# The latent-attention stage of a two-layer kernel in another order: one block projection ahead of the first scores, the first rotations shared by two engines, banks and steps dealt otherwise

## The reference, cut to what matters

```python
proj = u @ ab_w_in[e]                        # c_q | c_kv | k_rope_in | block q, k, v
q  = rmsnorm(c_q, q_norm_g) @ w_uq           # per head 64 plain + 32 rotated columns
kv = rmsnorm(c_kv, kv_norm_g) @ w_ukv        # per head 64 key + 64 value columns
q_rope, k_rope = rope(q[..., 64:], pos), rope(k_rope_in, pos)   # k_rope is shared by all heads
def rope(x):  # x1, x2: the halves of the 32 columns
    return concat([x1 * cos - x2 * sin, x1 * sin + x2 * cos])
logits = (q_nope @ k_nope.T + q_rope @ k_rope.T) * scale       # causal
out = softmax(logits) @ v                    # then @ ab_w_out, feed-forward, layer 1 (stick-breaking), feed-forward
```

## Time and profile before

| | us |
|---|---|
| median of the runs | 1307.0 |
| lowest, highest | 1306.68, 1309.34 |
| the profiled execution, its own time | 1307.3 |
| its span, first to last instruction | 1305.5 |
| PE busy in the span | 1266.4 |
| mean granted clock of TensorE | 0.991 |
| latent stage, first query product of head 2 to scores 7 (62.79 to 151.50) | 88.7 |
| PE busy in that stretch | 74.3 |

### The profile page before, as it was taken

The page is one execution under the profiler, slowest core; times in us unless marked ns, Lnnn a source line. Parts: engine busy times, 40 slices in busy tenths (PEclk is TensorE's granted clock), DMA queues, the critical chain, the costliest instruction groups (busy, mean ns, idle before and its releaser), DMA issues.

```text
span 1305.5 us, 17382 instructions
## 1 busy us (share of the span) xinstructions
PE 1266.4 (97%) x6487; PEld 1067.4 (82%) x6487; DVE 723.8 (55%) x928; ACT 553.0 (42%) x883; POOL 217.5 (17%) x198
## 2 busy tenths in 40 slices
PE   6979899999999999999999999999999999999997
PEld 5767788889888888888898888888988888888885
DVE  4677655528545545422258889884765545452223
ACT  5456666546422222222246565565542222232112
POOL 1532200026111111100042000002521111110002
PEclk9989999999999999999999999999999999999999
DMA  5412222132333333333322221213133333332331
GB/s 165 127 52 59 79 73 73 38 92 66 113 97 96 96 96 96 89 102 91 93 77 65 64 66 55 74 49 97 58 105 97 96 96 97 97 114 93 89 90 65
DMA packets 190502, 112.33 MB, mean 86 GB/s; under 512 B 13696, under 2 KB 184773, under 8 KB 190446
## 3 DMA queue, kind: packets, MB, share of 16 engines
q1 hardware_dynamic: 188636, 106.81, 28.2%
q0 software_dynamic: 640, 2.10, 0.6%
q10 hardware_dynamic: 1170, 2.66, 0.5%
HBM read 109.43 MB, written 4.74 MB: 87 GB/s over the span
## 4 chain that ended last, share of the span: by engine, by line
PE 85%; DVE 8%; ACT 3%; issue 2%; POOL 1%; DMA 0%; POOLq 0%; ACTq 0%; DVEq 0%; SPq 0%
PE banks L432 27%; PE banks L434 26%; PE banks L433 26%; PE banks L1724 1%; PE banks L1631 1%; DVE w_lo L427 1%; PE banks L1455 1%; PE banks L1695 1%; DVE logits L1417 1%; ACT logits L1428 1%; DVE tf L698 1%; DVE probsT_lo L1467 1%; POOL residual L769 0%; DVE stick_lo L1708 0%; DVE u_lo L708 0%
## 5 line engine op out<-in xcount | busy, mean ns | idle before, releaser
L427 DVE TENSOR_TENSOR w_lo<-w_raw,w_hi 128x1024 fp32r<-128x1024 f32 (+3 forms) x200 | 289.8, 1449 | 272.5 <-ACT w_hi L420 272.3
L432 PE MATMUL banks<-u_hi,w_hi 128*128 128x512 f32 (+1 forms) x1112 | 424.1, 381 | 5.6 <-DVE w_lo L427 4.3
L434 PE MATMUL banks<-u_hi,w_lo 128*128 128x512 f32 (+1 forms) x1112 | 419.9, 378 | 0.0
L433 PE MATMUL banks<-u_lo,w_hi 128*128 128x512 f32 (+1 forms) x1112 | 419.8, 377 | 0.0
L420 ACT ACTIVATE w_hi<-w_raw 128x1024 fp32r<-128x1024 f32 (+3 forms) x200 | 206.6, 1033 | 262.0 <-PE banks L434 261.7
L432 PEld LDWEIGHTS banks<-u_hi,w_hi 128*128 128x128 f32 x1112 | 211.0, 190 | 44.5 <-issue 3.9
L434 PEld LDWEIGHTS banks<-u_hi,w_lo 128*128 128x128 f32 x1112 | 211.0, 190 | 38.5
L433 PEld LDWEIGHTS banks<-u_lo,w_hi 128*128 128x128 f32 x1112 | 211.1, 190 | 36.7
L901 POOL TENSOR_TENSOR up<-up,gate 128x512 f32<-128x512 f32 x44 | 71.9, 1634 | 375.7 <-DVE up L927 358.3
L882 ACT ACTIVATE gate<-gate 128x512 f32<-128x512 f32 x44 | 27.8, 632 | 202.3 <-DVE gate L923 202.3
L602 POOL TENSOR_TENSOR sq_sum<-sq_sum,sq_tile 128x512 f32<-128x512 f32 x14 | 18.4, 1317 | 362.6 <-ACT block_out L583 362.6
(11 more groups left out here) (246 smaller groups left out, 1807.6 us busy)
## 6 DMA issues: line engine op xcount, KB each, us to landing
w_raw<-in_ffn_w_gate_up_dram SPq DMA_DIRECT2D x88, 512.0 KB, 3.7
w_raw<-in_ffn_w_down_dram SPq DMA_DIRECT2D x30, 512.0 KB, 3.6
w_raw<-in_sb_w_qkv_dram SPq DMA_DIRECT2D x24, 512.0 KB, 3.7
w_raw<-in_ab_w_in_dram SPq DMA_DIRECT2D x17, 512.0 KB, 3.7
w_raw<-in_ffn_w_down_dram SPq DMA_DIRECT2D x16, 448.0 KB, 3.6
w_raw<-in_ab_w_out_dram SPq DMA_DIRECT2D x8, 512.0 KB, 3.8
w_raw<-in_sb_w_out_dram SPq DMA_DIRECT2D x8, 512.0 KB, 3.8
bias_by_distance<-bias_rows ACTq DMA_DIRECT2D x1, 2560.0 KB
```

The lines of the kernel that those rows point to most:

```text
L427: dve.tensor_tensor(wl[:, c.slot, 0:w], raw[:, c.slot, 0:w], wh[:, c.slot, 0:w].bitcast(F32), ALU.subtract).then_inc(w_lo, 1)
L432: nc.tensor.matmul(o, lh, rh, start=start, stop=False, skip_group_check=True)
L433: nc.tensor.matmul(o, lh, rl, start=False, stop=False, skip_group_check=True)
L434: return nc.tensor.matmul(o, ll, rh, start=False, stop=stop, skip_group_check=True)
```

## The change

It touches the latent stage alone; from step 5 on the items of PE stand as before.

1. The first block projection, ("bq", 4), called x0, moves from slot b of step 0 to ahead of scores 0. ("bk", 4) and ("bq", 5) move to slot c of steps 0 and 2, step 4 has none, and the values' projection comes to slot b. The queries of head 2 move from ahead of scores 0 to behind it. The chunks are loaded in the new order.
2. The first three rotations (shared key part, heads 0 and 1) are shared: POOL keeps the product with cos, DVE takes the product with sin and the sum.
3. The shared key part is rotated and split once, on rows 64 to 95; ACT copies both parts to rows 32 to 63 of the two buffers for odd heads. Before, POOL wrote both row ranges, ACT rounded three times and DVE subtracted three times.
4. The keys of the two heads of a pair are rounded and subtracted apart (`odd_key_act`, `odd_key_dve`), the odd one later, with semaphores of their own.
5. Banks of the first eight items: 7, 3, 4, 5, 6, 3, 4, 7.
6. In steps 0, 2, 4 (`latent_step`) and 1, 3 (`keys_of`) ACT and DVE do the same work in another order: exponentials of head hh+1 come behind the keys where keys are due, and the rounding of the probabilities ahead of them.

The diff, cut:

```diff
-    names = [("cq", 0), ("ck", 0)]
-    for p in range(1, MLA_PAIRS):
-        names += [("cq", p), X_IN_LATENT[p - 1], ("ck", p)]
+    names = []
+    for p in range(MLA_PAIRS):
+        names += [("cq", p), ("ck", p)] + ([X_IN_LATENT[p]] if p in X_IN_LATENT else [])
...
-            steps.append([g[2], block_item(X_IN_LATENT[p]), g[3]])
+            steps.append([g[2], g[3], block_item(X_IN_LATENT[p + 1]) if p + 1 in X_IN_LATENT else None])
...
+    items = [q0, k0, q1, v0, x0, q2, vt0, k1] + [it for step in steps for it in step if it is not None]
+    vector_items = [k0, q0, q1, vt0, x0, k1, q2]
...
+        def rope_sin_dve(dve, number, rows=ROPE_ROWS):
+            dve.wait_ge(rp_sw, number + 1)
+            nc.vector.tensor_tensor(rt[rows, 0, :], rt[rows, 0, :], cs[rows, 1, :], ALU.mult).then_inc(rp_sin, 1)
+        def rope_sum_dve(dve, x, number, rows=ROPE_ROWS):
+            dve.wait_ge(rp_cos, number + 1)
+            dve.wait_ge(rp_sin, number + 1)
+            nc.vector.tensor_tensor(x[rows, :], rt[rows, 0, :], rt[rows, 1, :], ALU.add).then_inc(rp_done, 1)
...
-            return (7, 3, 4, 5, 6, 3, 7)[n] if n < 7 else P_BANK
+            return (7, 3, 4, 5, 6, 3, 4, 7)[n] if n < 8 else P_BANK
...
 (ACT, ahead of the steps)
+            load_functions(act, EXP_SET)
             act.wait_ge(rp_done, 1)
+            act.activation(mq[2][ROPE_ROWS, 0, :], k_rope[ROPE_ROWS, :], ACT.Copy).then_inc(kr_hi, 1)
+            item_act(act, k0)
+            item_act(act, q0)
+            odd_key_act(act, k0)
+            item_split_act(act, v0)
+            act.wait_ge(kr_lo, 1)
+            for b in (1, 2):
+                act.activation(mq[2][ODD_ROPE, b, :], mq[2][ROPE_ROWS, 0, :].bitcast(F32), ACT.Copy)
+                act.activation(mq[3][ODD_ROPE, b, :], mq[3][ROPE_ROWS, 0, :].bitcast(F32), ACT.Copy)\
+                    .then_inc(kr_odd, 1)
+            item_split_act(act, x0)
+            item_act(act, q1)
             exp_act(act, 0)
+            item_act(act, vt0)
             norm_act(act, 0)
...
 (ACT, steps 0, 2, 4)
+                if latent_step(hh):
+                    probs_act(act, hh)
+                    if keys_of(hh - 1):
+                        exp_act(act, hh + 1)
+                    norm_act(act, hh + 1)
+                    item_act(act, a)
+                    item_split_act(act, b)
+                    item_split_act(act, c)
+                    exp_act(act, hh + 2)
+                    item_act(act, c)
...
 (DVE, steps 0, 2, 4)
+                if latent_step(hh):
                     item_scale(dve, a)
+                    probs_dve(dve, hh)
+                    item_split_dve(dve, slots_of_step(hh - 1)[0] if hh else q2)
+                    den_dve(dve, hh + 1)
+                    item_scale(dve, b)
+                    if hh and not keys_of(hh - 1):
+                        o_dve(dve, hh // 2 - 1)
+                    scores_dve(dve, hh + 2)
+                    odd_key_dve(dve, keys_of(hh - 1))
+                    item_lo(dve, a)
+                    item_split_dve(dve, b)
+                    item_split_dve(dve, c)
+                    item_scale(dve, c)
+                    item_lo(dve, c)
...
 (PE, ahead of the steps)
-            for n in (2, 3, 5):
-                item_pe(pe, items[n])
+            for it in (q1, v0, x0):
+                item_pe(pe, it)
             scores_pe(pe, 0)
-            item_pe(pe, items[4])
+            item_pe(pe, q2)
+            item_pe(pe, vt0)
             scores_pe(pe, 1)
-            item_pe(pe, items[6])
+            item_pe(pe, k1)
```

More of the change, by code:

```diff
@@ L1156, in rope_rows_pool @@
             nc.gpsimd.tensor_tensor(rt[rows, 1, :], x[rows, :], cs[rows, 0, :], ALU.mult).then_inc(rp_cos, 1)
+        def rope_rows_pool(pool, x, number, scaled, rows=ROPE_ROWS):
+            rope_cos_pool(pool, x, number, scaled, rows)
             pool.wait_ge(rp_sw, number + 1)
@@ L1272, in keys_first, with latent_step, keys_of @@
             return (c, b) if b is not None and b[0] == "mq" else (b, c)
+        def latent_step(hh):
+            return hh % 2 == 0 and hh < 2 * MLA_PAIRS - 2
+        def keys_of(hh):
+            c = slots_of_step(hh)[2] if hh >= 0 else k1
+            return c if c is not None and c[0] == "mk" else None
         def item_split_act(act, it):
@@ L1299, in item_act @@
                 act.wait_ge(pj_read, read_at[it[:3]])
-                for rows, b in mk_dst(p):
-                    ins = act.activation(mq[2][rows, b, :], scaled_tile(it)[rows, :], ACT.Copy)
-                ins.then_inc(pj_hi, 1)
+                rows, b = mk_dst(p)[0]
+                act.activation(mq[2][rows, b, :], scaled_tile(it)[rows, :], ACT.Copy).then_inc(pj_hi, 1)
                 return
@@ L1363, in item_lo, with odd_key_act, odd_key_dve @@
             nc.vector.tensor_tensor(lo, scaled_tile(it)[rows, :], hi.bitcast(F32), ALU.subtract).then_inc(pj_lo, 1)
+        def odd_key_act(act, it):
+            rows, b = mk_dst(it[1])[1]
+            act.activation(mq[2][rows, b, :], scaled_tile(it)[rows, :], ACT.Copy).then_inc(k_odd_hi, 1)
+        def odd_key_dve(dve, it):
+            rows, b = mk_dst(it[1])[1]
+            dve.wait_ge(k_odd_hi, it[1] + 1)
+            nc.vector.tensor_tensor(mq[3][rows, b, :], scaled_tile(it)[rows, :], mq[2][rows, b, :].bitcast(F32),
+                                    ALU.subtract).then_inc(k_odd_lo, 1)
         def item_pool(pool, it):
@@ L2122, in _ @@
                     item_split_act(act, a)
-                if hh + 2 < NH0:
+                if hh + 2 < NH0 and not keys_of(hh):
                     exp_act(act, hh + 2)
```

157 lines of the change are left out of this document (79 added, 78 removed).

## The result

The changed kernel took 1297.4 us in the median of six runs (1295.98 to 1297.95), the kernel before 1307.3 beside it: a ratio of 0.992 with an interval of 0.9907 to 0.9934. It is faster, as forecast, but by 9.9 us and not by 14.8, and 1297.4 lies 0.9 us above the range. The profiled execution took 1295.98.

What follows compares the result with a forecast made beforehand. PE's waits on the chain product, scale, rotate, round, subtract, with DVE in every link, bound the stage; 68.6 us of work, 4.5 of waits and restarts gave a 14.8 us gain: 1307.0 - 14.8 = 1292.2, range 1289.5 to 1296.5.

Steps and rivals of the forecast that it cites:

- bound of 20.1 us: 88.7 us from head 2's queries to scores 7, less 68.6 at full speed: the most any order can give.
- 2.7 us booked for the clock: Scores 0 and 1 of the kernel before: time lost in all by running at a granted clock of 0.5.
- The start: Up to scores 0: operands ready 1.7 us earlier, scores 0 at 68.05 behind x0 without a wait, at full clock.
- The step that failed: Head 2's queries to scores 1: queries end 72.05, transposition 72.4, scores 1 74.35, the wait of 2.23 us gone.
- rival B: The clock falls again at waits of 0.5 and 1.9 us around pair 1's keys, costing 1.5: 1293.7 us; chance 0.23.
- Waits that are left: PE waits: pair 1's keys 0.5, probabilities 0 1.9, scores 2 0.2, probabilities 5 1.4, scores 7 0.5; together 4.5 us.
- The port: Two-input DVE instructions that meet POOL run in turns; if merely shared, a weight part ends 0.5 earlier: 1291.8 us.
- Steps 1 to 4: Waits of 0.66, 0.73 and 1.17 us go, a step pair lasts 22.85; probabilities 5 wait 1.4.
- rival C: Hand-offs slower than laid: narrowly avoided waits return and POOL wins another turn in step 4, 5.1 us: 1297.3; chance 0.20.
- D: Little gained: ACT stands at the chunk for q2 and k1, loaded three us late: 1295 us; chance 0.03.
- E: Slower than before: waits of steps 0 to 4 keep PE at 1.2 GHz, up to 1342 us; chance 0.03.
- PE without waits after: Behind scores 7: no new wait of PE, as in the old trace, so the whole gain arrives at the end.

Runs made afterwards that it cites:

- b1: The kernel before, with eight idle products on PE ahead of scores 0 and eight ahead of scores 1; 1308.0 us.
- e1: The changed kernel, but the transposition of pair 0's values waits only for the read of its own tile, not for x0's scaling; 1294.3 us.
- e7: The changed kernel with its wait kept and fourteen idle products on PE inside it, ahead of the transposition of pair 0's values; 1295.0 us.
- e8: e1 with DVE scaling the next query product behind the reading of the scores again in steps 1 and 3; 1296.0 us.
- e10: e1 with the two keys of a pair rounded and subtracted together again, as before the change; 1296.1 us.
- e6: The changed kernel with e1's edit, x0 scaled first, reciprocals earlier, step 4's weight part later and head 6's exponentials later on ACT; 1292.3 us.
- e9: e6 with the weight part of the chunk behind moved after the values' halves on ACT and DVE in the last steps; 1289.9 us.
- e11: e5 with 16 idle products on PE ahead of scores 1, inside its wait of 4.72 us; 1294.2 us.
- b2: The kernel before, with DVE scaling the next query product ahead of reading the scores in odd steps; 1311.3 us.
- e5: e1 with x0 back in its step: block projections in steps 0, 2 and 4, head 2's queries again ahead of scores 0; 1296.0 us.
- e2: The changed kernel with its wait kept, but DVE scales x0 ahead of head 2's queries; 1291.8 us.

## Why the prediction was wrong, point by point

- **What bounds the kernel, and the most that can be won.** The reading of the earlier trace rows held: most of what went is waiting (9.0 of 11.6 us). The bound of 20.1 us is the stage less its work at full clock, and it stands. But its parts are no prices of their own: the 2.7 us booked for the clock bring nothing when they alone are taken away (b1: 0.0 at x5), since a wait beside them takes them up.
- **The start.** Right: scores 0 at 68.49 behind x0 without a wait and at full clock (68.05 forecast; the stage began 0.33 later here). The sin products and sums on DVE took 0.68 us each, near the lower bound of 0.61 that was taken and far from 1.9. DVE reached the read of scores 0 at 70.57 and not at 69.2, since q1's sum and the odd key stood ahead of it; probabilities 0 come 0.5 late in e1 (23.63 against 78.3 - 55.2 = 23.1), and this is the likely cause; no run isolates it.
- **The step that failed** is this one: "The queries of head 2 run 70.0 to 72.05, the transposition to 72.4, scores 1 to 74.35." The queries of head 2 did end near there (72.59, with the stage 0.33 later). For the transposition only its operand was asked about, not what its instruction waits for. That is a count of scalings, it includes x0's, and the prediction itself had x0 scaled at 75.5 and used that time for nothing but the softmax. By its own list vt0 starts at 75.5, and the transposition, scores 1 and the keys (0.35 + 1.95 + 1.37) end at 79.2, behind the 78.3 of the softmax: 0.9 us on the path, and 1.5 more with rival B's price for a fall, so 1294.6. What was measured is a wait of 3.94 us ahead of vt0 that costs 3.4 us at x5, 1.9 of them through the clock (e1, e7). Two of the signs of being wrong that the prediction named came: a granted clock of 0.50 after 76, and a new wait after scores 7.
- **Rival B** was the right mechanism in the wrong place. It put the fall behind the short waits around the keys of pair 1; there the clock stayed at 1.00 in e1, with ten transpositions behind the 1.58 us. It fell behind the 3.94 us. The Trainium skill (TensorE: Matmul & The Clock Gate, section "Part 4: PE-mode transpose") doesn't count transpositions as busy in the same way, which would have made a fall likelier behind them; no run here shows one.
- **Waits that are left.** 0.5, 1.9, 0.2, 1.4 and 0.5 were forecast; e1 has 0.68, 1.58, 0, 1.27 and 0.16. In the changed kernel the 1.9 are covered by the longer wait ahead.
- **The port.** Pricing in turns held. The weight part at 74.71 lasts 1.07 us: POOL's cos product ends at 75.23, and 0.61 more is 75.84. In step 4 it was to end 7.8 us after the start of probabilities 4 and did (next fence: 136.15, less 128.37). The Trainium skill (SBUF — State Buffer, section "SBUF: two separate sides") says that the two lock each other out for a whole instruction, and both numbers agree with it.
- **Steps 1 to 4.** A step pair lasts 22.85 us, from 96.73 to 119.58, as forecast, and PE has no wait in it. The waits that rival C brings back stayed away; e8 and e10 show that they were close, 0.5 to 0.8 us a hand-off.
- **The other rivals.** D didn't come: ACT rounded the chunks for q2 and k1 at 64.94 and 67.87 without waiting for a load. E didn't either: the clock was back at 1.00 from 82 us on. Its working holds a slip, for by its own price, 1 us lost for each us of work at half clock, some 15 us of such work and not 30 would eat the gain.
- **Behind scores 7.** "PE without waits after" failed by 0.93 us. In the sum it stood as "the old trace has no wait of PE there", which an order that is 12 us earlier doesn't inherit. DVE and ACT of the changed kernel:

```profile
134.68 1.47 DVE L430 TENSOR_TENSOR w_lo<-w_raw,w_hi 128x1024 fp32r<-128x1024 f32 x1
136.07 0.17 DVE L1473 RECIPROCAL rden<-den 128x4 f32<-128x4 f32 x1
...
142.41 0.76 DVE L1379 TENSOR_TENSOR v_lo<-banks,v_hi 128x256 fp32r<-128x256 f32 x2 [1.18 <-ACT v_hi L1323]
```

```profile
138.62 1.04 ACT L423 ACTIVATE w_hi<-w_raw 128x1024 fp32r<-128x1024 f32 x1
139.57 0.71 ACT L1467 ACTIVATE logits<-logits,neg_max 128x512 f32<-128x512 f32 x1
...
141.75 0.36 ACT L1322 ACTIVATE v_hi<-banks 128x256 fp32r<-128x256 f32 x1
```

The rounding of the last values stands behind a weight part and head 6's exponentials on ACT, and x5 waits for the subtraction that follows. e6, which moves the exponentials, still has 0.81 us there; e9, which moves the weight part too, has no wait.

**The account.** Gain at scores 7 forecast: 14.8. Measured 96.30 - 84.63 = 11.7, 3.1 short; with the wait at x5 (0.93, and some 0.2 for the restart behind it) 10.55. e1, without vt0's extra wait, has 15.1 at scores 7. The time of the changed kernel follows: 1307.3 - 10.55 = 1296.75, against 1297.4 measured; 0.7 is within what start and rest vary by.

## What to carry to other kernels

When items change places, every wait that is written as a position in a list changes its meaning. Go through the waits of each moved item one by one, write down which instruction satisfies each, and put its time into the schedule; that the operand is ready is not enough. A wait that goes is worth what the next wait on that path leaves of it (e6: 1.9 of 2.7 us; e11: 0.8 of 2.4; b1: nothing, though the clock was kept up for two heads), and a stretch whose work comes earlier has to be looked through for new waits even where its order is untouched.

## What the runs showed of the hardware

The granted clock was 0.50 behind single waits of 2.20 (before), 2.69 (b1), 3.12 and 3.15 (b2), 3.94 (changed) and 4.72 us (e5), and stayed at 1.00 behind those of 1.84 and 1.58 (e2, e1). At about 2.2 us the same list came out in two ways. In the kernel before, the first product behind the wait of 2.20 us already ran slow (0.80 us). In b2, whose list is the same up to there, the first one behind 2.19 us took 0.50, and 0.50 was granted only from the next microsecond on. There the clock was also still low at the keys of pair 1, which ran at full clock in the kernel before.

```profile
69.24 0.50 PE L432 MATMUL banks<-mla_k_hi,mla_q_hi 128*128 128x512 f32 x1 [2.19 <-DVE mla_q_lo L1363]
...
80.33 0.77 PE L432 MATMUL banks<-ckv_hi,w_hi 128*128 128x512 f32 x1 [1.77 <-DVE w_lo L427]
```

So where exactly the clock falls is not fixed by the list alone. Idle products in the wait kept it up in e7 and e11, and brought 1.9 and 0.8 us; in b1 they brought nothing, since a wait for DVE's weight part followed. What was not expected is that one and the same measure is worth all, half or none of its price by the place it is put in.
